# The end of mixer B's output projection and the next block's first projections, multiplied by halves of the tokens

## What is computed

```python
x = x + g_x * yx                      # yx = (o * silu(z)) @ w_out of mixer B
return rms_norm(x, final_norm_g)      # end of the first block
...
hN = _rmsnorm(x, norm_g[l])           # start of the second block, on that result
p = _split_in(hN @ w_in[l])
mq = jax.nn.silu(_causal_dwconv(p["m_q"], conv_q_w[l], conv_q_b[l]))
mk = jax.nn.silu(_causal_dwconv(p["m_k"], conv_k_w[l], conv_k_b[l]))
```

## Time and profile before

| | us |
|---|---|
| median of three runs | 1568.41 (1567.42 to 6650.71) |
| the profiled execution, its own time | 1569.0 |
| its span, first to last instruction | 1567.3 |
| TensorE busy | 1510.2 (96%) |
| VectorE, ScalarE, GpSimd busy | 747.7, 642.4, 689.9 |
| mean granted TensorE clock | 0.985 of full |

### The profile page before, as it was taken

One profiled execution on the slowest core, in us unless ns is written; L12 is line 12 of the kernel. 1 busy time (PEld: TensorE's weight loads), 2 busy tenths in 40 slices (PEclk: granted clock), 3 DMA queues, 4 the chain that ended last, 5 costly groups with the idle time before them and its releaser, 6 DMA issues.

```text
span 1567.3 us, 25094 instructions
## 1 busy us (share of the span) xinstructions
PE 1510.2 (96%) x9930; PEld 1219.1 (78%) x9930; DVE 747.7 (48%) x1643; ACT 642.4 (41%) x1369; POOL 689.9 (44%) x657
## 2 busy tenths in 40 slices
PE   5999999999899999999998899999999999999997
PEld 3877777777687888787876777878787877777887
DVE  5344545445534334434455475735443564454154
ACT  5345444444532533333334453435332444443331
POOL 3444444444532533433434445455355435554462
PEclk9999999999999999999999999999999999999999
DMA  9211111121023222322231322122121231111221
GB/s 394 76 54 55 55 55 35 57 73 55 1 108 108 81 75 88 108 82 81 83 106 32 130 88 81 54 83 106 54 99 64 81 108 55 54 55 55 88 94 61
DMA packets 23284, 128.21 MB, mean 82 GB/s; under 512 B 2432, under 2 KB 4736, under 8 KB 9216
## 3 DMA queue, kind: packets, MB, share of 16 engines
q1 hardware_dynamic: 23024, 126.35, 22.6%
q10 hardware_dynamic: 144, 0.26, 0.1%
HBM read 124.50 MB, written 2.10 MB: 81 GB/s over the span
## 4 chain that ended last, share of the span: by engine, by line
PE 88%; DVE 4%; ACT 2%; POOL 2%; issue 2%; DMA 1%; POOLq 0%; DVEq 0%; SPq 0%; ACTq 0%
PE PS L1588 17%; PE PS L1590 17%; PE PS L1589 17%; PE PS L1679 7%; PE PS L1669 7%; PE PS L1705 7%; PE PS L1581 3%; PE PS L1582 3%; PE PS L1583 3%; PE PS L1601 1%; PE PS L1759 1%; PE PS L1751 1%; POOL WL L2638 1%; DVE sm L2298 1%; PE PS L1626 0%
## 5 line engine op out<-in xcount | busy, mean ns | idle before, releaser
L2638 POOL TENSOR_TENSOR WL<-W,WH 128x512 fp32r<-128x512 f32 x308 | 413.1, 1356 | 325.0 <-ACT WH L1867 324.9
L1588 PE MATMUL PS<-HX,WH 128*128 128x512 f32 (+1 forms) x1008 | 408.8, 406 | 8.3 <-POOL WL L2638 3.1
L1589 PE MATMUL PS<-LX,WH 128*128 128x512 f32 (+1 forms) x1008 | 388.7, 386 | 0.0
L1590 PE MATMUL PS<-HX,WL 128*128 128x512 f32 (+1 forms) x1008 | 388.6, 386 | 0.0
L1588 PEld LDWEIGHTS PS<-HX,WH 128*128 128x128 f32 x1008 | 191.0, 189 | 54.7 <-issue 17.2
L2696 POOL TENSOR_SCALAR AR<-AR,sm 128x768 f32<-128x768 f32 (+4 forms) x160 | 112.6, 708 | 249.7 <-DVE sm L2317 248.0
L1590 PEld LDWEIGHTS PS<-HX,WL 128*128 128x128 f32 x1008 | 190.7, 189 | 39.4
L1589 PEld LDWEIGHTS PS<-LX,WH 128*128 128x128 f32 x1008 | 191.4, 190 | 33.4 <-issue 2.6
L1867 ACT CAST WH<-W 128x512 fp32r<-128x512 f32 x320 | 187.8, 621 | 32.4 <-PE PS L1583 13.2
L2298 DVE TENSOR_REDUCE sm<-PS 128x1 f32<-128x512 f32 (+4 forms) x192 | 144.9, 755 | 55.1 <-PE PS L1669 51.3
L1953 ACT ACTIVATE AR<-PS,sm 128x768 f32<-128x768 f32 (+4 forms) x160 | 114.9, 722 | 104.2 <-DVE sm L2303 86.1
(11 more groups left out here) (284 smaller groups left out, 2475.9 us busy)
## 6 DMA issues: line engine op xcount, KB each, us to landing
W<-in_wu SPq DMA_DIRECT2D x98, 1024.0 KB, 4.8
AR<-in_wu SPq DMA_DIRECT2D x8, 1024.0 KB, 10.4
AR<-in_biasb SPq DMA_DIRECT2D x32, 256.0 KB, 2.8
XX<-in_xt SPq DMA_DIRECT2D x2, 1024.0 KB, 6.3
XC<-in_xt SPq DMA_DIRECT2D x1, 1024.0 KB, 12.8
out<-XX SPq DMA_DIRECT2D x2, 512.0 KB, 3.0
out<-XX SPq DMA_DIRECT2D x4, 256.0 KB, 2.2
C<-in_cc SPq DMA_DIRECT2D x1, 642.5 KB, 9.6
```

The lines of the kernel that those rows point to most:

```text
L1588: e.matmul(o, wh, xh, start=(k == 0), stop=False)
L1589: e.matmul(o, wh, xl, start=False, stop=False)
L1590: t = e.matmul(o, wl, xh, start=False, stop=(k == 7))
L2638: e.tensor_tensor(WL[:, d, a:z], W[:, n % 2, a:z], WH[:, d, a:z].bitcast(F32), ALU.subtract).then_inc(*s_wl_pool.by(n, q))
```

## The change

Blocks 4 to 7 of bout are multiplied in two halves of 256 tokens: m = 4 to 7 for the first half, then again for the second. Both norms run by halves (parts 0 and 1), and their factors are made inside the second half's groups. The second norm's factor comes from one power, of the sum of both mean squares with the small constants worked in, in place of a power that waits for the first norm's; the first norm's own power moves behind it, since only `norm2_x` much later needs it. VectorE's list mixes the second half's residuals and adds with the scaling of the first half's blocks. The gates and `mq` head 0 are multiplied by halves too, the second halves interleaved by block k. `gw` and `mq` are marked done only behind all of this. To have halves of tokens in bout, the gated activations are put into natural order where their parts are made (`by_rows`), not at the residual. The transposes of the last modulation unit move from behind block 4's 24 matmuls to behind 6.

```diff
         def parts_b(k):
-            parts("p", k, 0, zB[:, k, :], [(s_gated, ("b", k)), (s_proj, ("bv", 3, 5) if k < 4 else ("bz", 7))], "pool" if k % 2 == 0 else "dve")
+            parts("p", k, 0, zB[:, k, :].rearrange("p (w r) -> p r w", r=8), [(s_gated, ("b", k)), (s_proj, ("bv", 3, 5) if k < 4 else ("bz", 7))], "pool" if k % 2 == 0 else "dve")
...
-        norm("c", ar, X_ONLY, first, lambda k, p: [(s_res, ("bout", k, 0))])
-        norm("d", ar, X_ONLY, first, lambda k, p: [(s_res, ("bout", k, 0))], "fg", rcol2)
+        residual_of = lambda k, p: [(s_res, ("bout", k, 0) if k < 4 else ("bout", k, "half", p))]
+        norm("c", ar, X_HALVES, first, residual_of)
+        norm("d", ar, X_HALVES, first, residual_of, "fg", rcol2)
         fgg = smc(8)
         do("gain2")
-        out_proj("bout", 1, XONLY, True, "p", ["c", "d"], [None, MA[15]], third=FB)
-
-
-
-        ar = Arena()
-        hb2 = Rows(ar(4096), ar(2048))
-        close("c", 0, ONE)
-        norm_sums("d", 0, ONE)
-        do("norm2_rs")
-        R2 = bank(ONE.take("R2", (s_r2, ("h", 7))))
-        rbroad("d", 0, R2)
-        do("norm2_h", 0)
+        mod_ = out_proj("bout", 1, XONLY, "p", ["c", "d"], [None, MA[15]], third=FB, units=2)
+
+
+
+        hb2 = Rows(AR[:, 0:4096], AR[:, 4096:6144])
+
+        def factor(half):
+            norm_sums("c", half, ONE)
+            norm_sums("d", half, ONE)
+            do("norm2_rs", half)
+
+        def h_scaled(half, *ks):
+            for k in ks:
+                do("norm2_h", k, half)
+
+        def h_parts(half, *ks):
+            for k in ks:
+                parts("h", k, half, hb2.at(k, HALF * half, HALF * half + HALF), [(s_r2, ("h", k, half))], "pool" if k % 2 else "dve")
+
+        bun = [Unit("bout", 2), Unit("bout", 3, split_now=False)]
+
+        def out_half(m, half, *between):
+            g = ("bout", m, "half", half)
+            o = bank(ONE.take(g, (s_res, g)))
+            at = 0
+            for ks, act in between:
+                run(pj(g, bun[m // 2 - 2], 0, T, 128 * (m % 2), "p", o, range(at, ks), half))
+                at = ks
+                act()
+            run(pj(g, bun[m // 2 - 2], 0, T, 128 * (m % 2), "p", o, range(at, 8), half))
+            if half and m % 2:
+                bun[m // 2 - 2].done(s_proj, *g)
+            return lambda: do("residual", *g), lambda: squares(["c", "d"], m, half)
+
+        def finish(*acts):
+            for act in acts:
+                act()
+
+        def all_pieces():
+            while pieces:
+                tick(True)
+
+        finish(*out_half(4, 0, (2, lambda: next(mod_, None))))
+        finish(*out_half(5, 0))
+        all_pieces()
+        finish(*out_half(6, 0))
+        finish(*out_half(7, 0))
+        finish(*out_half(4, 1, (5, lambda: factor(0))))
+        do("norm_rs", "c", 0)
+        R2 = bank(ONE.take("R2", (s_r2, ("h", 7, 1))))
+        r, q = out_half(5, 1, (4, lambda: rbroad("d", 0, R2)))
+        r()
+        h_scaled(0, 0, 1)
+        q()
+        h_parts(0, 0)
+        h_scaled(0, 2)
+        h_parts(0, 1)
+        h_scaled(0, 3)
+        r, q = out_half(6, 1)
+        r()
+        h_parts(0, 2)
+        h_scaled(0, 4)
+        q()
+        h_parts(0, 3)
+        h_scaled(0, 5)
+        h_parts(0, 4)
+        r, q = out_half(7, 1)
+        r()
+        h_scaled(0, 6)
+        q()
+        h_parts(0, 5, 6)
+        h_scaled(0, 7)
+        h_parts(0, 7)
+
+        un = Unit("gw")
+        gwo = bank(ONE.take("gw", (s_gr, ())))
+        gwu = un.n
+
+        def gate_sums(half, *ks):
+            for k in ks:
+                do("m_gate_sums", half, k)
+
+        def low_by(engine):
+            quick[0] = engine == "dve"
+            if pieces:
+                tick(True)
+            quick[0] = False
+
+        unq = Unit("mq", 0, split_now=False)
+        gate_sums(0, 0, 1, 2, 3, 4)
+        low_by("dve")
+        factor(1)
+        gate_sums(0, 5, 6, 7)
+        low_by("dve")
+        led = {}
+
+        def query_part(m, half, ks):
+            g = ("mq", 0, m) if half else ("mq", 0, m, "first")
+            run(pj(g, unq, 0, T, 128 * m, "h", led[m], ks, half))
+
+        for m in range(2):
+            if m:
+                ONE.n += 1
+            led[m] = bank(ONE.take(("mq", 0, m, "first"), (s_cp, ("mq", 0, m))))
+            before["mq", 0, m] = []
+        low_by("dve")
+        low_by("pool")
+        query_part(0, 0, range(8))
+        rbroad("d", 1, R2)
+        query_part(1, 0, range(8))
+        do("norm_rs", "c", 1)
+        h_scaled(1, 0)
         for k in range(KC):
             if k < KC - 1:
-                do("norm2_h", k + 1)
-            parts("h", k, 0, hb2.at(k, 0, T), [(s_r2, ("h", k))], "pool" if k % 2 else "dve")
-        flush()
+                h_scaled(1, k + 1)
+            h_parts(1, k)
+        for k in range(KC):
+            gate_sums(1, k)
+            for m in range(2):
+                query_part(m, 1, (k,))
+        un.done(s_proj, "gw")
+        unq.done(s_proj, "mq", 0, 1)
...
         def conv(key, hd):
-            un = Unit(key, hd)
+            begun_ = key == "mq" and hd == 0
+            un = None if begun_ else Unit(key, hd)
             for m in range(2):
                 g = (key, hd, m)
-                o = bank(ONE.take(g, (s_cp, g)))
-                run(pj(g, un, 0, T, 128 * m, "h", o))
+                if begun_:
+                    groups[g] = Group(g, unq.n, False, 0, T, 128 * m, 128, "h", led[m])
+                else:
...
-            un.done(s_proj, *g)
+            if not begun_:
+                un.done(s_proj, *g)
...
                     rbroad("c", 0, R1)
+                    rbroad("c", 1, R1)
...
+            def m_gate_sums(half, k):
+                if k == 0 and half == 0:
+                    free(w, "gw")
                 part = PART[gwu]
...
-            def norm2_rs():
-                r1, r2 = norms["c"].r[:, 0:4], norms["d"].r[:, 0:4]
-                w.wait_ge(*s_sums("d", 0))
-                w.wait_ge(*s_rs("c", 0))
-                e.scalar_tensor_tensor(out=r2, in0=norms["d"].sums[0][:, 0:4], scalar=1.0 / D, in1=r1, op0=ALU.mult, op1=ALU.mult).then_inc(*s_var.by("d", 0))
-                w.wait_ge(*s_var("d", 0))
-                e.tensor_tensor(r2, r2, r1, ALU.mult).then_inc(*s_var.by("d2"))
-                w.wait_ge(*s_var("d2"))
-                e.tensor_scalar(r2, r2, EPS, None, ALU.add).then_inc(*s_var.by("d3"))
+            def norm2_rs(p):
+                r2 = norms["d"].r[:, 2 * p:2 * p + 2]
+                w.wait_ge(*s_sums("c", p))
+                e.tensor_scalar(r2, norms["c"].sums[p][:, 0:2], EPS / D, EPS * EPS, ALU.mult, ALU.add).then_inc(*s_eps.by(p))
+                w.wait_ge(*s_sums("d", p))
+                w.wait_ge(*s_eps(p))
+                e.scalar_tensor_tensor(out=r2, in0=norms["d"].sums[p][:, 0:2], scalar=1.0 / D, in1=r2, op0=ALU.mult, op1=ALU.add).then_inc(*s_var.by("d", p))
 
...
-                r, r1 = norms[name].r[:, i:i + 1], norms["c"].r[:, i:i + 1]
-                if name == "d":
-                    e.tensor_scalar(dg[i % 4], c("id"), r, r1, ALU.mult, ALU.mult).then_inc(*s_dg.by(name, i))
-                else:
-                    e.tensor_scalar(dg[i % 4], c("id"), r, None, ALU.mult).then_inc(*s_dg.by(name, i))
+                e.tensor_scalar(dg[i % 4], c("id"), norms[name].r[:, i:i + 1], None, ALU.mult).then_inc(*s_dg.by(name, i))
...
+            def norm2_h(k, half):
+                lo, hi = span_of("h", half)
+                w.wait_ge(*s_rb("d", 2 * half + 1))
                 w.wait_ge(*s_fgg())
-                e.scalar_tensor_tensor(out=hb2.at(k, 0, T), in0=xT.at(k, 0, T), scalar=fgg[:, k:k + 1], in1=R2, op0=ALU.mult, op1=ALU.mult).then_inc(*s_r2.by("h", k))
+                e.scalar_tensor_tensor(out=hb2.at(k, lo, hi), in0=xT.at(k, lo, hi), scalar=fgg[:, k:k + 1], in1=R2[:, lo:hi],
+                                       op0=ALU.mult, op1=ALU.mult).then_inc(*s_r2.by("h", k, half))
```

104 lines of the change are left out of this document (56 added, 48 removed).

## The result

The changed kernel takes 1583.97 us (median of 4) and the kernel before 1567.91: +16 us. The ratio is 1.0109, with a 95% interval from 1.0097 to 1.0121, so the change is slower, by about 1%. One of the four times of the kernel before was 6650.71; without it their median is 1567.42. The forecast was 1576.7, and the range ended at 1582.5. The profiled execution spans 1583.1 us against 1567.3: +15.8.

What follows compares the result with a forecast made beforehand. The prediction took TensorE's own list as the bound. It summed -1.7 us for the earlier end of `mq`, +7.8 waiting before `mk` and +2.2 for a cold clock to +8.3: 1576.7 us, range 1569.5 to 1582.5.

Steps and rivals of the forecast that it cites:

- the second halves of gates and both blocks, 72 x 0.12 = 8.6: At the end of `mq`: the second halves of the gates and both `mq` blocks are 72 half products, 8.6 us.
- the change does not do what it says: VectorE's list might put the first half's scaling behind bout all the same; counted as part of the third rival.
- `parts_b` with a stride: 0 to 0.5, taken as 0: Ahead of bout: reading the parts with a stride costs 0 to 0.5 us, taken as 0 because TensorE is busy there.
- Products of halves: bout, gates and `mq` at 0.12 us per half product: 43.1 us with small work, which would win 10.3.
- Waits (a) to (c): In bout: transposes behind 6 products, 1.4 us; block 6 on unit 3's weights, 1.4; sums 0.2 and block 5's broadcast 0.9.
- VectorE's list: Behind bout: 8.4 us of VectorE work, 0.3 of waits, 2.2 of hindrance by GpSimd; first half's last scaling at 903.3.
- the second rival: VectorE is not hindered by GpSimd and `mk` starts at full clock: +3.4 us, 1571.8; chance 0.15.
- the third rival: All ten VectorE operations are held 0.5 us longer by GpSimd, with a colder clock: about +10.4 us, 1578.8; chance 0.12.
- the fourth rival: TensorE stays at half clock from about 900 until `mq` is done, and sums take 4.15: +14 us, 1582.5; chance 0.10.
- The wait in front of `mk`: `mk`'s casts stand behind gates, convolution copies and first tanh, so TensorE stands 7.8 us, from 5.6 to 9.6.
- The clock behind it: After that idle stretch `mk` starts at clock 0.50, losing 2.2 us, from 0 to 2.8.
- The first rival: The wait in front of `mk` is absorbed by shorter later waits: -1.7 us, 1566.7, down to 1558.1; chance 0.08.

Runs made afterwards that it cites:

- true_halves: The changed kernel with the second halves of the query projection multiplying 256 tokens instead of 512: 1580.62 us, ratio 1.0092 to the kernel before.
- before_natural: The kernel before with only the strided `parts_b` and `residual` of the changed one, nothing halved: 1572.18 us against 1566.53, ratio 1.0032.
- transposes_back: pieces_ahead with the last modulation unit's transposes again behind block 4's 24 half products, not 6: 1572.16 us, ratio 1.0032 to the kernel before.
- keys_early: The changed kernel with `mk`'s four weight pieces entered right behind `mq`'s products, its 512-token products kept: 1584.41 us, ratio 1.0114 to the kernel before.
- pieces_ahead: true_halves with `mk`'s pieces ahead of `mq`'s last block (low parts by VectorE), the values' between `mq`'s convolutions: 1572.16 us, ratio 1.0032 to the kernel before.
- order_by_vector: transposes_back with natural token order made by VectorE's output write and gate product, so casts read in a row: 1570.62 us, ratio 1.0016 to the kernel before.
- one_power: The kernel before with only the second norm's factor from one power, nothing halved: 1565.33 us against 1566.41, ratio 0.9994.
- tail_halves: The kernel before with only what follows bout's block 7 halved, one power, key and value pieces entered as in pieces_ahead: 1577.2 us, ratio 1.007.
- tail_mended: tail_halves with the first norm's powers behind the second factor and two query weight pieces ahead of GpSimd's second power: 1569.72 us, ratio 1.0018 to the kernel before.

## Why the prediction was wrong

The sign, the mechanism of the largest term and its size were right; the time is 16 above before where 8.3 was forecast. Two terms of the sum failed, and they come first:

- **"the second halves of gates and both blocks, 72 x 0.12 = 8.6"** failed. They take 13.84, since 48 of the 72 have 512 tokens: what `mq`'s first halves computed is computed again. true_halves shows it: 5.4 off the way from block 4 to the end of `mq`, which was forecast at 51.7 and took 57.9. The prediction had "the change does not do what it says" as a rival, but looked for it in VectorE's list and not in TensorE's.
- **"`parts_b` with a stride: 0 to 0.5, taken as 0"** failed. Alone it costs 5.6 (3 to 7, before_natural). TensorE is not simply busy ahead of bout: it waits for ScalarE at the end of the attention, 2.49 with the strided casts for 1.14, and the casts stand in that list. In the shown pair of traces it is 2.2, with the first column's variation in it; the profiled execution of the kernel before, 1569.0 by its own time, is itself above the medians of 1566 to 1568.
- **Products of halves** at 0.12: right. bout takes 28.9 from block 4 for a forecast of 28.5. **Waits (a) to (c)**: 1.3 (0.9 at the transposes, 0.4 at the low part), 1.5 and 1.0 for 1.4, 1.4 and 0.9. But (a) is no loss by itself (transposes_back).
- **VectorE's list**: the first half's last scaling ends 34.5 behind block 4's start for 33.7. The adds took 0.38 each ahead of GpSimd's low parts of weights and 1.0 beside them, in the changed kernel:

```profile
896.30 0.75 DVE L2294 TENSOR_TENSOR AR<-AR 128x256 f32<-128x256 f32 x2
...
897.95 1.29 POOL L2757 TENSOR_TENSOR WL<-W,WH 128x512 fp32r<-128x512 f32 x1
898.49 1.04 DVE L2340 TENSOR_TENSOR LX<-AR,HX 128x256 fp32r<-128x256 f32 x1
899.21 1.48 POOL L2757 TENSOR_TENSOR WL<-W,WH 128x512 fp32r<-128x512 f32 x1
...
899.84 1.13 DVE L2294 TENSOR_TENSOR AR<-AR 128x256 f32<-128x256 f32 x1
...
900.65 0.93 POOL L2787 TENSOR_TENSOR LX<-AR,HX 128x256 fp32r<-128x256 f32 x1
900.89 0.96 DVE L2294 TENSOR_TENSOR AR<-AR 128x256 f32<-128x256 f32 x1
```

Each of the three slow operations of VectorE ends 0.27 to 0.29 behind the end of the GpSimd instruction that was running when it began (899.24, 900.69, 901.58); the three others that were held (902.17, 904.14, 905.14) end 0.28 behind one too. So what one loses is not a fixed 0.5 but the rest of that instruction, and an operation that meets GpSimd idle loses nothing. Over the ten operations it came to 3.0 for the 2.2 taken; the second rival (0) and the third (5) fall. "0.5 for the clock" was 1.5 by the window from 908.14: 2.96 us at 0.50. In the second halves behind it (915.83 to 929.67) the clock was 1.00, so the fourth rival falls too, though the time lies nearest to its own.
- **The wait in front of `mk`**: 7.4 for 7.8, ended by a low part of GpSimd as forecast. **The clock behind it**: 2.45 for 2.2. keys_early takes both away and shows what the prediction did not see: what the wait covers. Without it the values wait in its place, so that mending it alone gains nothing; mended together with what came to light behind it, it was worth 8.5 (pieces_ahead against true_halves).
- A row misread, and it is the one that would have warned of this: the prediction takes the two casts at 924.84, behind the tanh, for `mk`'s third and fourth. A unit has four pieces, and `mk`'s are the two at 914.30 and the two at 918.88, so those at 924.84 are the first two of the values. The sum does not use them; but they say that the values' pieces too are cast behind a tanh, and so come late when the tanh does.
- The first rival (absorbed later): -0.8 behind the values. It fell.
- Slips in its arithmetic that change little: 0.0133 is the price of a pair of halves (0.24 less 0.227), and "0.12 less half of 0.227" is half of that; its steps give 7.6 for the wait in front of `mk` where it took 7.8; and ten operations held 0.5 make H 906.1, where the third rival has 905.7.

With 5.2 for the redundant columns and 2.2 for the stride added to 8.3, the forecast would have been 15.7, for 15.8 in the trace. That it closes so well is in part luck: by the runs the stride costs more (5.0 to 5.6) and the redundant columns less once the wait behind them is counted (2.7 to 3.4). What stays open is how the price of the stride divides between the longer wait and the lower clock around it: the wait is 1.3 longer, and 15 us at 0.77 do 1.8 us less work than at 0.89 (an estimate from the two windows), but no run changes one without the other.

## What to carry to other kernels

Before pricing products by a plan's intention, read the shape of each from the instructions that are emitted: a record that is written twice, with an argument left out, here doubled the width of 48 of them, and the output stayed right. Before taking a reordering of data as free, look at whom its engine serves in that stage, not at its share of busy time: ScalarE is busy for 41% of the span, and four casts that took 0.57 us longer each cost 5. And when a stall is taken away, ask which pieces were prepared in its shade; here the wait of the keys, once mended, showed that of the values, and this one, once mended, showed smaller ones in the unit behind, with 3 us left behind the values.

## What was not expected of the hardware

- ScalarE's cast of 128x512 takes 0.62 us when it reads in a row and 1.19 when it reads every eighth element; VectorE's product of two SBUF operands takes 0.71, and 1.16 when one of the two is read so (order_by_vector). VectorE's strided residual out of PSUM takes the same 0.75 either way (rows 891.98 of before, 868.20 of the changed kernel).
- From 830 to 845, around the wait of the attention's end, the granted clock was 1.00 in one_power and tail_halves, 0.89 in before and tail_mended, and 0.77 in all nine kernels that read or write with a stride there. TensorE's wait was 1.14 or 1.15 in the first four, 1.59 in order_by_vector and 2.48 to 2.52 in the other eight. So even a wait longer by half a microsecond stood beside a clock as low as the longest did; but the first four show that with equal waits the clock can differ too, and no run changes the wait alone.
- Two diagonals of 128x128 took 0.48 us with GpSimd idle, 0.47 beside the start of a power of GpSimd's (892.54 in the changed kernel), and 2.50 beside its low parts (tail_halves).
